# Moving the taps of a 31-tap convolution from the attention heads into the projection ahead of them

## The reference

```python
CONF_CONV = 31
def conformer_conv(a, g, w, bias, ln_g, ln_b):
    u = a * jax.nn.sigmoid(g)
    u = dwconv(u, w) + bias                  # 31 taps along the rows, 256 channels
    return jax.nn.silu(layer_norm(u, ln_g, ln_b))

def layer(x, xc, ...):
    h = rms_norm(x, n1) * (1 + sc1) + sh1
    a_b, a_c, a_h, b_v, b_g, c_q, c_k, c_v, d_q, d_k, d_v = split_proj(h @ w_in)
    ya = short_conv_mixer(a_b, a_c, a_h, conv_a)
    yb = conformer_conv(b_v, b_g, conv_b, conv_b_bias, cln_g, cln_b)
    yc = window_attention(rope(c_q), rope(c_k), c_v, ..., sink)
    yd = global_attention(rope(rms_norm(d_q)), rope(rms_norm(d_k)), d_v, ...)
    x_new = x + g1 * (jnp.concatenate([ya, yb, yc, yd], axis=-1) @ w_out)
    h2 = rms_norm(x_new, n2) * (1 + sc2) + sh2
    return x_new + g2 * expert_choice_ffn(h2, router, w_gate, w_up, w_down)
```

## Time and profile before

| | us |
|---|---|
| median of three runs | 3186.76 |
| lowest, highest | 3182.98, 3188.02 |
| the profiled execution | 3168.38 |
| its span on the core | 3166.6 |
| PE busy in the span | 2946.7 (93%) |
| DVE busy | 1102.6 (35%) |
| ACT busy | 737.7 (23%) |
| POOL busy | 383.6 (12%) |

### The profile page before, as it was taken

One profiled execution on the slowest core, in us unless ns is written; L12 is line 12 of the kernel. 1 busy time (PEld: TensorE's weight loads), 2 busy tenths in 40 slices (PEclk: granted clock), 3 DMA queues, 4 the chain that ended last, 5 costly groups with the idle time before them and its releaser, 6 DMA issues.

```text
span 3166.6 us, 50031 instructions
## 1 busy us (share of the span) xinstructions
PE 2946.7 (93%) x21634; PEld 1852.5 (59%) x21634; DVE 1102.6 (35%) x1948; ACT 737.7 (23%) x1393; POOL 383.6 (12%) x497
## 2 busy tenths in 40 slices
PE   6999987899999898996988888999999999999998
PEld 3655555555545464553433335888865568678887
DVE  4124755111111344742322224222334463232232
ACT  3113751000000223630000003222223362222232
POOL 2022620222221211501000000000000000000000
PEclk9998998999999998997999999999999999999999
DMA  9930044899999610049999994212321202232130
GB/s 377 368 134 1 0 159 199 336 410 411 406 412 405 260 56 0 1 168 387 423 422 423 423 422 169 106 56 78 115 70 54 80 8 80 80 113 88 46 146 27
DMA packets 138512, 627.05 MB, mean 198 GB/s; under 512 B 12640, under 2 KB 19872, under 8 KB 83008
## 3 DMA queue, kind: packets, MB, share of 16 engines
q1 hardware_dynamic: 122064, 577.67, 45.5%
q0 software_dynamic: 16240, 46.27, 4.3%
HBM read 607.45 MB, written 16.45 MB: 197 GB/s over the span
## 4 chain that ended last, share of the span: by engine, by line
PE 42%; DMA 11%; DVE 2%; ACT 1%; issue 1%; SPq 0%; POOL 0%; DVEq 0%; ACTq 0%; POOLq 0%
PE bank L975 20%; DMA slots<-in_w_up_dram 10%; PE bank L1555 8%; PE bank L1743 4%; PE bank L1432 3%; PE bank L1659 3%; PE bank L1299 2%; PE bank L1676 1%; PE bank L1453 1%; PE bank L1687 0%; PE bank L1482 0%; PE bank L1677 0%; SPq L926 0%; PE bank L1076 0%; PE bank L1077 0%
## 5 line engine op out<-in xcount | busy, mean ns | idle before, releaser
L1432 PE MATMUL bank<-slots,HT 128*32 128x256 f32 x8192 | 477.2, 383 | 53.6 <-DMA slots<-in_w_gate_dram 26.6
L1432 PEld LDWEIGHTS bank<-slots,HT 128*32 128x32 f32 x8192 | 265.1, 111 | 269.9 <-issue 64.9
L975 PE MATMUL bank<-hT_high,chunk_high 128*128 128x512 f32 (+2 forms) x736 | 285.7, 388 | 6.2 <-DVE hT_low L2531 6.2
L975 PE MATMUL bank<-hT_high,low_slots 128*128 128x512 f32 (+2 forms) x736 | 287.7, 391 | 0.0
L975 PE MATMUL bank<-hT_low,chunk_high 128*128 128x512 f32 (+2 forms) x736 | 286.1, 389 | 0.0
L2125 ACT ACTIVATE arena<-bank 128x512 f32<-128x512 f32 x32 | 19.1, 597 | 756.8 <-PE bank L1432 435.0
L975 PE MATMUL bank<-slots,HT 128*128 128x512 f32 (+4 forms) x544 | 178.3, 487 | 1.4 <-ACT done_mark L2381 1.4
L2904 DVE TENSOR_TENSOR arena<-bank,arena 128x512 f32<-128x512 f32 x32 | 22.1, 692 | 439.9 <-ACT arena L2125 439.9
L975 PEld LDWEIGHTS bank<-hT_high,chunk_high 128*128 128x128 f32 x736 | 139.5, 190 | 36.6 <-DVE hT_low L2531 6.4
L975 PEld LDWEIGHTS bank<-hT_low,chunk_high 128*128 128x128 f32 x736 | 139.2, 189 | 32.1 <-issue 0.2
L975 PEld LDWEIGHTS bank<-hT_high,low_slots 128*128 128x128 f32 x736 | 139.0, 189 | 29.5
(11 more groups left out here) (462 smaller groups left out, 4828.8 us busy)
## 6 DMA issues: line engine op xcount, KB each, us to landing
slots<-in_w_gate_dram SPq DMA_DIRECT2D x128, 1024.0 KB, 19.8
slots<-in_w_up_dram SPq DMA_DIRECT2D x128, 1024.0 KB, 21.7
arena<-in_w_down_dram SPq DMA_DIRECT2D x80, 1024.0 KB, 24.4
arena<-in_ada_w_dram SPq DMA_DIRECT2D x48, 1024.0 KB, 9.0
X<-in_w_down_dram SPq DMA_DIRECT2D x32, 1024.0 KB, 17.8
slots<-in_w_in_dram SPq DMA_DIRECT2D x15, 2048.0 KB, 8.5
slots<-in_ffn_w_gate_dram SPq DMA_DIRECT2D x10, 2048.0 KB, 7.8
slots<-in_ffn_w_up_dram SPq DMA_DIRECT2D x10, 2048.0 KB, 8.1
```

The lines of the kernel that those rows point to most:

```text
L975: mm = pe.matmul(out_, lhsT, rhs, start=(n == 0), stop=(n == len(pairs) - 1))
L1432: mm = pe.matmul(bank[32 * j:32 * j + 32, 2 + n, 256 * g:256 * g + 256], xT[:, 64 * k + 32 * g:64 * k + 32 * g + 32], columns(w[:, c, :], ...
```

## The change

Three tables say how much of the convolution runs in qkv. Behind the work of tile i DVE makes DVE_TAPS[layer][i] taps (57 of 62 in layer 0, 29 of 31 in layer 1), and ACT makes ACT_TAPS[layer][i] products (34 of 62, 22 of 31), which POOL adds behind its memsets. The rest runs in attend as before. The sum goes to conv_sum, which lies where the values were before they were copied (V), not to HT.

The mean, the subtraction, the squares and the mean of squares move from conv_out into attend, into the group `groups[-ahead]` (the seventh of eight, and the last of four): the mean behind the mix of step 1, the mean of squares behind that of step 4, the squares behind the exponentials of step 3. PE waits there for a mark by DVE behind its last tap (conv_summed) and for POOL's last add. conv_out keeps the root, the reciprocal, the product and the silu. The transpose of the modulation moves from bank 5 to bank 6.

The query buffer becomes a list with the second kind of attention first, so that the slot of the first half of the output weight is free once the scores of all but the last `ahead` groups are made. SP loads that half then, and the second half, as before, behind the last mix.

```diff
+CONV_MEANS, CONV_SQUARES = (1, 4), 3
+DVE_TAPS = ((10, 10, 10, 10, 11, 6), (5, 6, 6, 6, 4, 2))
+ACT_TAPS = ((0, 6, 8, 8, 8, 4), (0, 6, 6, 6, 4, 0))
...
-        pool_taps = mod.rearrange("p a b -> p (a b)")[:, SEQ:4 * SEQ].rearrange("p (a b) -> p a b", a=3)
-        products = h_tok.rearrange("p a b -> p (a b)").rearrange("p (a b) -> p a b", a=4)
+        pool_taps = h_tok.rearrange("p a b -> p (a b)")[:, 0:3 * SEQ].rearrange("p (a b) -> p a b", a=3)
+        products = [h_tok[:, 1, D - SEQ:D], mod[:, 1, D - SEQ:D], flat_probs[:, 4 * SEQ:5 * SEQ], flat_probs[:, 5 * SEQ:6 * SEQ]]
+        conv_sum = V.rearrange("p a b -> p (a b)").rearrange("p (c n) -> p c n", c=2)
+        taps_left = {}
...
-                if stage.name == "w_out":
-                    sp.wait_ge(sem["mixed"], attended)
+                    groups = stage.facts["groups"]
+                    ahead = 2 if stage.layer == 0 else 1
+                    first_scored = stage.at("score_full", sum(len(one.parts) for group in groups[:-ahead] for one in group.steps))
                 for j, (make, (b, use)) in enumerate(stage.units):
                     unit = stage.first_unit + j
+                    if stage.name == "w_out" and j == 0:
+                        sp.wait_ge(sem["score_full"], first_scored)
+                    if stage.name == "w_out" and j == 1:
+                        sp.wait_ge(sem["mixed"], attended)
...
+                def conv_mean(n):
+
+                    if n == 0:
+                        pe.wait_ge(sem["shift_done"], st.at("shift_done", len(groups)))
+                        pe.wait_ge(sem["conv_summed"], st.at("conv_summed", 1))
+                        pe.wait_ge(sem["tap_added"], st.at("tap_added", st.signals["tap_added"]))
+                        source = conv_sum
+                    else:
+                        pe.wait_ge(sem["squared"], st.at("squared", 2))
+                        pe.wait_ge(sem["free4"], at_bank(st, 4, 0))
+                        source = u_sq
+                    parts = [(0, SEQ)] + ([(SEQ, NTOK)] if st.layer == 0 else [])
+                    for q, (lo, hi) in enumerate(parts):
+                        product(bank[:, 4 + q, 0:hi - lo], [(mean_of[:, :], source[:, c, lo:hi]) for c in range(2)],
+                                sem["full4"] if q == len(parts) - 1 else None)
...
                         mix(one)
+                        if group is groups[-ahead] and n in CONV_MEANS:
+                            conv_mean(CONV_MEANS.index(n))
...
-                mean(0, [HT[:, 2, :], HT[:, 3, :]])
                 for i in range(2):
                     project_part(out_stage, i, 0, OUT_WHOLE)
                 kinds = mod_kinds(st.layer)
                 pe.wait_ge(sem["mods_loaded"], st.at("mods_loaded", 16 * kinds))
-                pe_may_fill(pe, st, 5, 0)
-                pe.transpose(bank[:, 5, 0:16 * kinds], mod_rows2[0:16 * kinds, :], ident[0:16 * kinds, 0:16 * kinds]).then_inc(sem["full5"], 1)
-                pe.wait_ge(sem["squared"], st.at("squared", 2))
-                mean(1, [u_sq[:, 0, :], u_sq[:, 1, :]])
...
                     if i:
                         take_turned(i - 1)
+                    tap_some(ACT_TAPS[st.layer][i])
...
+                        if group is groups[-ahead] and n == 0:
+                            for _ in ready_taps:
+                                pass
+                        if group is groups[-ahead] and n == CONV_SQUARES:
+                            for c in range(2):
+                                if c == 0:
+                                    act.wait_ge(sem["centered"], st.at("centered", 1))
+                                else:
+                                    act.wait_ge(sem["free4"], at_bank(st, 4, 0))
+                                act.activation(u_sq[:, c, 0:tokens], conv_sum[:, c, 0:tokens], ACT.Square).then_inc(sem["squared"], 1)
...
-                act.wait_ge(sem["full6"], at_bank(st, 6, 1))
-                act.activation(u_rstd[:, 0:n], bank[:, 6:8, :].rearrange("p b n -> p (b n)")[:, 0:n], ACT.Sqrt, bias=eps[:, :]).then_inc(sem["free6"], 1)
-                for step_of in range(4, OUT_STEPS[st.layer]):
+                act.wait_ge(sem["full4"], at_bank(behind, 4, 1))
+                act.activation(u_rstd[:, 0:n], flat_bank[:, 4 * BANK:4 * BANK + n], ACT.Sqrt, bias=eps[:, :]).then_inc(sem["free4"], 1)
+                for step_of in range(2, OUT_STEPS[st.layer]):
...
                     ins.then_inc(sem["qk_ready"], 1)
                     dve.wait_ge(sem["qk_ready"], st.at("qk_ready", i + 1))
+                    tap_some(l, DVE_TAPS[l][i])
...
-                    tap_some(5 if units else 12)
-                tap_some(3 * TAPS_B)
+                    if group is not groups[-ahead]:
+                        tap_some(l, 5)
+                        continue
+                    tap_some(l, 3 * TAPS_B)
+                    step.wait_for(0)
+                    dve.memset(done_mark[:, 1:2], 0.0).then_inc(sem["conv_summed"], 1)
+                    dve.wait_ge(sem["full4"], at_bank(st, 4, 0))
+                    for c in range(2):
+                        dve.tensor_tensor(conv_sum[:, c, 0:tokens], conv_sum[:, c, 0:tokens], flat_bank[:, 4 * BANK:4 * BANK + tokens],
+                                          ALU.subtract).then_inc(sem["free4" if c else "centered"], 1)
                 outcome(groups[-1])
...
+                add_taps(st, sum(ACT_TAPS[l]), TAPS_B * len(parts))
+
+            def add_taps(st, first, last):
+
+                l = st.layer
+                for n in range(first, min(last, st.signals["tap_added"])):
+                    part, k = n // TAPS_B, n % TAPS_B
+                    lo, hi = (0, SEQ) if part == 0 else (SEQ, NTOK)
+                    dst = conv_sum[:, 0, lo:hi]
+                    pool.wait_ge(sem["tap_made"], st.at("tap_made", n + 1))
+                    if k:
+                        pool.wait_ge(sem["tap_added"], st.at("tap_added", n))
+                    other = dst if k else conv_vec[:, 0, l, 0:1].broadcast_to([P, hi - lo])
+                    pool.tensor_tensor(dst, other, products[n % 4][:, 0:hi - lo], ALU.add).then_inc(sem["tap_added"], 1)
...
                 step(pool.memset(sink_sel[HD:HD + 1, HD:2 * HD], 1.0))
+                add_taps(stage_behind(st), 0, sum(ACT_TAPS[st.layer]))
```

More of the change, by code:

```diff
@@ L1901, in conv_in, with made_taps @@
                         high_columns(st, c + IN_RING[st.layer])
+            def made_taps(st):
+                made = 0
+                for part, (lo, hi) in enumerate([(0, SEQ)] + ([(SEQ, NTOK)] if st.layer == 0 else [])):
+                    for k in range(TAPS_B):
+                        if made >= 4:
+                            act.wait_ge(sem["tap_added"], st.at("tap_added", made - 3))
+                        at_k = part * (SEQ + 2 * PAD_B) + k
+                        act.activation(products[made % 4][:, 0:hi - lo], conv_b_in[:, 0, at_k:at_k + hi - lo], ACT.Copy,
+                                       scale=conv_b_w[:, st.layer, 0, k:k + 1]).then_inc(sem["tap_made"], 1)
+                        made += 1
+                        yield
             def qkv(st):
```

124 lines of the change are left out of this document (48 added, 76 removed).

## The result

The changed kernel took 3222.26 us (median of five runs, 3213.07 to 3227.67), the kernel before 3186.76: a ratio of 1.0108, 95% interval 1.0090 to 1.0127, or 34 us more with 29 to 40 as its interval. The forecast was 3216, range 3193 to 3240. Slower, as forecast, and by 5 to 6 us more than the sum said.

What follows compares the result with a forecast made beforehand. PE was taken to bound the stages, with DVE's tile chains and DVE-POOL exclusion limiting free room in the projection. Layer 0 +16.5 and layer 1 +13.1 gave +29.6 on the median 3186.8: 3216 us, range 3193 to 3240.

Steps and rivals of the forecast that it cites:

- Contention in the projection: Queries' projection: each POOL add overlapping DVE work costs DVE 0.93 us; +21 us in layer 0, +13 in layer 1.
- The deduction of 5 us for adds that fall into DVE's waits: Projection, layer 0: adds falling into DVE's waits or one-input steps are free, 5 us off the 27.9 us of adds.
- The 5 us added for mutual waits: Projection, layer 0: ACT and DVE wait on one another, ACT's next tile copy standing behind eight products; 5 us added.
- the prediction's warning: Projection: if ACT's copy behind eight products also stops PE's banks, PE idles between tiles too; no size given.
- the 6 taps behind tile 5 lie beside take-over work: Projection, layer 0: DVE's six taps behind the last tile run beside other work; no cost put on them.
- Layer 1: Queries' projection of layer 1: 22 taps and 22 adds delay the last tile to 1251 against 1238.07, +13 us.
- -5 and +5.7: Attend, layer 0: shortened PE waits and one lower-clock spell lost, -5 us; means and squares moved in, +5.2 and +0.5.
- The wait for DVE's mark behind all taps: Last heads of attend: PE waits for conv_summed and POOL's last add before the mean; costed at nothing.
- Head of conv_out: Start of conv_out without the means: 6.5 us instead of 11.7 in layer 0 (-5.2), 6.3 instead of 9.00 in layer 1 (-2.7).
- Lighter contention: Rival, projection: an add costs DVE half of 0.93 us because POOL gives way; 3193, up to 3200 us; chance 0.12.
- Whole exclusion: Rival, projection: tap and add fully exclude each other, 2.15 us a pair instead of 1.71, +23, 3239 us; chance 0.09.
- The other side: Rival: taps find idle time after all, 3182 us (0.10); if means also fill PE's gaps, 3173 us (0.07).

Runs made afterwards that it cites:

- the experiment on the means: Against the kernel with 64 and 31 early DVE taps where DVE makes all taps: means, subtraction and squares back at conv_out's head; 3177.08 us, ratio 0.9973.
- the kernel with memsets: Changed kernel with each POOL add in the queries' projection replaced by two memsets of the same tile, those taps left out of the sum; 3176.33 us, ratio 0.9976.
- two kernels whose stages nearly agree: Changed kernel with DVE making all taps, no ACT products or POOL adds: 3179.33 us; the same with more taps early (64 and 31): 3173.16 us.

## Why the prediction was right, and by how much it was off

**Contention in the projection: the right cause, the term 4 us too small in layer 0 and 3 in layer 1.** The sum had 0.93 us an add; measured is 0.98 in the latent tile above and 0.99 in the first context tile (269.09 to 286.90, 17.81 us, less 3.69 and 6.2 for chain and eleven taps, over eight adds). The deduction of 5 us for adds that fall into DVE's waits was wrong: ACT starts its products when the tile's root is done, and the eight adds begin at 233.17, beside the rotary products, so none falls on the reduction, the reciprocal or the wait. (That an add beside the reduction is free is so: the kernel without DVE's taps has the case.) The 5 us added for mutual waits were wrong as well, on the other side: 261.3 + 30 x 0.98 = 290.7, and DVE's last chain ends at 290.6. That the forecast's 289 came so near is in part luck, since the two wrong corrections cancel. And PE did idle between tiles, but for DVE's late chains, not because ACT's copies kept its banks, as the prediction's warning had it.

**The step "the 6 taps behind tile 5 lie beside take-over work" failed**, and it left out ACT's four products behind that tile. From the last turn to attend it is 7.6 us instead of 4.8. By the run without the six taps, 0.7 of these 2.8 us are DVE's; the other 2.1 are in ACT's timeline, the products and the copies behind them. With the turn's own delay of 22.1 the term is 24.9, not 21.

**Layer 1: +16 instead of +13**, the same mis-sized term: 1231.6 + 22 x 0.98 = 1253.2, 15.1 behind 1238.07; the last turn came 15.9 later than before, counted from the first copy.

**Attend: -5 and +5.7 in the sum, -0.5 to -4.2 together by the traces** (forecast +0.7). The two parts can be told apart in the windows of attend with the idle time behind, before and after (length, then PE's busy time first):

```profile
272.90:432.67 159.77, 141.70 (x432) 81.02 (x433) 102.34 (x135) 93.45 (x175) 86.51 (x86) 0.85 0.03 10
```

```profile
298.20:457.50 159.30, 146.72 (x448) 83.69 (x449) 64.72 (x81) 74.14 (x143) 40.38 (x52) 0.85 0.06 23
```

PE's busy time rose by 5.0 us and its idle time fell from 18.1 to 12.6, by 5.5, both close to the forecast. PE's waits for ACT's copies of the outcome are 1.8 us in all where the same view of before has 6.1, and the experiment on the means put 4.7 us on them. The two profiles of before differ by 3.6 us in this stage, nearly all of it idle time (142.20 us busy of 163.40 in the second). So the 5.0 is firm, and the gain in idle time is 5.5 or 8.6, by the profile it is taken against. In layer 1 I had +2.8 and it is 0 to 0.6. The wait for DVE's mark behind all taps, put at nothing, is nothing: no wait stands at the means in the changed kernel. One reading ahead of the sum was wrong: the helpers' 80 to 100 us in attend are not "nearly all the convolution's". Of the 102.3, 93.5 and 86.5 us of DVE, ACT and POOL in the first of these windows, taps, products and adds are 42.0, 34.5 and 66.9.

**Head of conv_out: right** (-5.0 and -2.4 for -5.2 and -2.7), PE's weight matmuls 6.05 us as estimated.

**The rivals.** Lighter contention is excluded by the 0.98. Whole exclusion put 2.15 us on a pair: 0.78 + 1.37; a pair of add and tap takes 0.78 + 0.98 = 1.76, so the two do overlap by some 0.4 us. Of that, 0.14 is POOL's own pause between two adds (the add shown above takes 1.26 us, the next one starts at 235.99). The other side (taps find idle time) is what happens for taps without adds: the kernel with memsets was 8 us faster than before. The prediction saw no way to a gain but adds under DVE's waits, while the cure was to have no adds.

The prediction's inner range, 3203 to 3231, does not follow exactly from its terms: 13 us to either side of 34 give 3203 to 3229, and 3 more for attend 3200 to 3232. The result lies inside either.

**Left open.** Why an add and DVE's operation overlap by the quarter of a microsecond that is left; and the 6 us between two kernels whose stages nearly agree.

## What to carry to other kernels

Before giving half of an elementwise job to GpSimd, measure what its instruction costs VectorE when both read two SBUF operands. Here an add costs 0.98 us of VectorE, more than the 0.78 of doing the whole tap on VectorE, so the helper was a loss wherever the two met. And read free room on an engine as the time to the moment its consumer needs it, with the work's price under contention in it: 57 taps alone went into the projection for nothing, 34 adds beside them cost 25 us. When a helper's instruction must run there, prefer one that only writes: the memsets cost VectorE nothing.

## What the runs showed of the hardware that I had not expected

- A short DVE operation pays as much as a long one: an add of 512 columns makes a rotary product of 192 columns 1.37 us long instead of 0.36, a tap of 256 columns 1.48 instead of 0.48, a tap of 512 columns 1.64 or 1.75 instead of 0.74. The cost goes by GpSimd's instruction, not by VectorE's. The whole chain of a tile is exposed, not the taps alone.
- A reduction, which reads one operand, took 0.55 us beside an add as without it.
- Two memsets of GpSimd in a row beside the same DVE work changed no DVE duration by more than 0.02 us.
- The stretch over the experts of layer 0, which the change does not touch, took 709.5 us in one execution and 724 to 727 in all the others, and a stretch of the second block 92 or 102 us with a granted clock of 1.00 or 0.86. The two profiles of the unchanged kernel before differ by 22.0 us of span (3166.6 and 3188.6).
